# A modulation matrix loaded 32 rows at a time into four partition blocks, and summed in 12 products instead of 48

## The reference, cut to what matters

```python
ada = (jax.nn.silu(c) @ ada_w[l] + ada_b[l])[:, None, :]      # c: (1, 1024), ada_w: (1024, 6144)
sh1, sc1, g1, sh2, sc2, g2 = jnp.split(ada, 6, axis=-1)
u = rms_norm_2(h, norm1_g[l]) * (1 + sc1) + sh1
...
h = h + g1 * (merged @ w_out[l])
u2 = rms_norm_2(h, norm2_g[l]) * (1 + sc2) + sh2
h = h + g2 * peer_layer(u2, ...)
```

## Time and profile before

| | us |
|---|---|
| median of 3 runs | 1569.6 (1567.91 to 1569.87) |
| the profiled execution, its own time | 1573.47 |
| the span of its trace | 1571.5 |
| TensorE busy in the span | 1459.9 (93%) |
| the 32 modulation adds on DVE | 67.6 busy, 26.5 idle before them |
| the 32 modulation loads, issue to landing (median) | 6.4 |

### The profile page before, as it was taken

The page is one execution under the profiler, slowest core; times in us unless marked ns, Lnnn a source line. Parts: engine busy times, 40 slices in busy tenths (PEclk is TensorE's granted clock), DMA queues, the critical chain, the costliest instruction groups (busy, mean ns, idle before and its releaser), DMA issues.

```text
span 1571.5 us, 22748 instructions
## 1 busy us (share of the span) xinstructions
PE 1459.9 (93%) x8272; PEld 1120.8 (71%) x8272; DVE 1049.8 (67%) x2170; ACT 546.4 (35%) x1128; POOL 563.6 (36%) x382
## 2 busy tenths in 40 slices
PE   8999999999999999999999999998988988888777
PEld 7999998767999999998989985444444443333333
DVE  6655376875734328998976468785858585858556
ACT  5444353363544436443134242221212121212114
POOL 2455428220344441001002234554545444444451
PEclk9999999999999999999999999999999998999999
DMA  9888958996999997999976969999999999999996
GB/s 365 312 329 317 348 217 338 315 326 241 407 372 371 376 376 294 374 398 342 362 281 226 401 244 403 404 427 427 427 427 426 427 427 427 427 427 427 426 428 267
DMA packets 99814, 571.91 MB, mean 364 GB/s; under 512 B 11536, under 2 KB 11664, under 8 KB 50448
## 3 DMA queue, kind: packets, MB, share of 16 engines
q1 hardware_dynamic: 61056, 298.15, 51.3%
q0 software_dynamic: 37520, 268.47, 40.7%
q10 hardware_dynamic: 1152, 4.16, 0.7%
HBM read 569.67 MB, written 135.27 MB: 449 GB/s over the span
## 4 chain that ended last, share of the span: by engine, by line
PE 57%; DMA 26%; DVE 6%; SPq 5%; POOL 3%; issue 2%; ACT 1%; ACTq 0%; POOLq 0%; DVEq 0%
DMA arena<-pairs,eidx 15%; PE ps L2727 10%; PE ps L2113 8%; PE ps L2112 8%; PE ps L2111 8%; DMA ring<-pairs,eidx 6%; PE ps L2504 5%; SPq L664 3%; PE ps L2200 2%; PE ps L2198 2%; PE ps L2199 2%; DMA arena<-in_ada 2%; POOL w_lo L754 2%; SPq L663 2%; PE ps L2619 2%
## 5 line engine op out<-in xcount | busy, mean ns | idle before, releaser
L2727 PE MATMUL ps<-arena 128*128 128x512 f32 x844 | 402.6, 626 | 69.1 <-ACT arena L1252 69.1
L2727 PEld LDWEIGHTS ps<-arena 128*128 128x128 f32 x844 | 165.8, 201 | 289.0 <-issue 192.8
L1965 DVE CUSTOM_DVE_ANT_0 arena<-arena 128x1024 f32<-128x1024 f32 x211 | 255.2, 1225 | 145.3 <-DMA arena<-pairs,eidx 144.1
L822 POOL DMA_INDIRECT arena<-pairs,eidx x210 | 244.3, 1163 | 257.1 <-PE ps L2727 208.4
L754 POOL TENSOR_TENSOR w_lo<-ring,w_hi 128x1024 fp32r<-128x1024 f32 x76 | 207.9, 2738 | 257.7 <-DVE w_lo L1305 171.3
L2111 PE MATMUL ps<-u_hi,w_hi 128*128 128x256 f32 (+1 forms) x912 | 259.4, 284 | 1.8 <-POOL w_lo L754 1.5
L2113 PE MATMUL ps<-u_hi,w_lo 128*128 128x256 f32 (+1 forms) x912 | 259.6, 285 | 0.0
L2112 PE MATMUL ps<-u_lo,w_hi 128*128 128x256 f32 (+1 forms) x912 | 259.2, 284 | 0.0
L842 ACT ACTIVATE w_hi<-ring 128x1024 fp32r<-128x1024 f32 x188 | 197.8, 1056 | 149.7 <-PE ps L2200 71.2
L2111 PEld LDWEIGHTS ps<-u_hi,w_hi 128*128 128x128 f32 x912 | 172.1, 189 | 3.2 <-issue 2.3
L2113 PEld LDWEIGHTS ps<-u_hi,w_lo 128*128 128x128 f32 x912 | 172.3, 189 | 0.0
(11 more groups left out here) (394 smaller groups left out, 2505.3 us busy)
## 6 DMA issues: line engine op xcount, KB each, us to landing
ring<-in_stream SPq DMA_DIRECT2D x121, 1024.0 KB, 7.0
pairs<-in_peer_u SPq DMA_DIRECT2D x128, 512.0 KB, 7.5
pairs<-in_peer_v SPq DMA_DIRECT2D x128, 512.0 KB, 8.6
arena<-in_ada SPq DMA_DIRECT2D x32, 768.0 KB, 6.4
arena<-in_stream SPq DMA_DIRECT2D x8, 1024.0 KB, 9.9
arena<-pairs,eidx POOLq DMA_INDIRECT x210, 19.7
h<-in_x_t SPq DMA_DIRECT2D x2, 544.0 KB, 4.7
ring<-in_stream SPq DMA_DIRECT2D x2, 512.0 KB, 7.1
```

Of the source, the lines that this page charges most:

```text
L822: pool.indirect_dma_start(slot_of(n), None, pairs, own).then_inc(landing(n)[0], 16)
L1965: dve.tensor_tensor_reduce(row, row, hf[:, n % HEAD_ROWS // TOPK, :], 1.0, 0.0, ALU.mult, ALU.add, dots[:, n % HEAD_ROWS:n % HEAD_ROWS + 1 ...
L2727: mm = pe.matmul(ps[:, Y_BANKS[j // TOPK] + half, :], diag[:, n % DIAGS, :], slot_of(n)[:, D + half * 512:D + half * 512 + 512], start=(hd ...
```

## The change

Each load now brings 32 rows with all their 6144 columns. It reads the same four arrays of one `kt`, but 32 rows of each, and puts the four quarters of the columns below each other: partition `32 j + r` gets quarter `j` of row `r`. So every partition holds 1536 columns of a row, as before, and the DVE instruction has the same size, 128 x 1536. All 32 adds go into one accumulator of 1536 columns, and each waits for the one before it. `silu_c` has 32 columns, since the scalar of a partition now depends on which 32 rows are loaded. Four small loads on SP's queue put `c` into that form. After the last add each column block of 128 holds, in four groups of 32 partitions, partial sums of four different results; TensorE takes them apart with 12 products by `quarter`, a matrix with a one where row // 32 equals the column. DVE adds the bias to all 48 columns at one place.

The diff, with the functions that it touches:

```diff
+ADA_ROWS = P // ADA_Q
 CONSTS = [("ident", P), ...,
-          ("ones", P), ("rot", P), ("cos", T), ("sin", T), ("neg_mask", P)]
+          ("ones", P), ("rot", P), ("cos", T), ("sin", T), ("neg_mask", P), ("quarter", WIDE)]
+    quarter = np.zeros((P, ADA_Q), np.float32)
+    quarter[np.arange(P), np.arange(P) // ADA_ROWS] = 1.0
+    put("quarter", quarter)
-        silu_c = sb("silu_c", [P, KT])
+        silu_c = sb("silu_c", [P, KT * ADA_Q])
-        ada_acc = view(ADA_Q, ADA_W)
+        ada_acc = view(ADA_Q, ADA_W // ADA_Q)
+        ada_flat = ada_acc.rearrange("p q w -> p (q w)")
+        place(ADA_Q * ADA_W)
             def load_ada(kt, q):
                 sp.wait_ge(ada_step, kt * ADA_Q + (q + 3))
-                n = kt * ADA_Q + q
-                src = a["ada"][n] if isinstance(n, int) else a["ada"][bass.ds(n, 1)].rearrange("o p w -> p (o w)")
+                quarters = slice(kt * ADA_Q, kt * ADA_Q + ADA_Q) if isinstance(kt, int) else bass.ds(kt * ADA_Q, ADA_Q)
+                src = a["ada"][quarters, q * ADA_ROWS:(q + 1) * ADA_ROWS, :]
                 sp.dma_start(ada_ring[:, q % 2, :], src).then_inc(ada_in[q % 2], 16)
+            c_rows = a["cols"][:, COL["c"]:COL["c"] + KT].rearrange("(q r) k -> r q k", q=ADA_Q)
+            for g in range(ADA_Q):
+                own = silu_c[g * ADA_ROWS:(g + 1) * ADA_ROWS, :].rearrange("r (q k) -> r q k", q=ADA_Q)
+                sp.dma_start(own, c_rows).then_inc(c_in, 16)
-            act.activation(silu_c[:, :], V("c", 0, KT), ACT.Silu).then_inc(silu_c_done, 1)
+            act.wait_ge(c_in, 16 * ADA_Q)
+            act.activation(silu_c[:, :], silu_c[:, :], ACT.Silu).then_inc(silu_c_done, 1)
-            act.wait_ge(ada_done, 4)
+            act.wait_ge(ada_done, 3)
             def ada_add(kt, q):
                 dve.wait_ge(ada_in[q % 2], kt * 32 + (q // 2 * 16 + 16))
-                dve.wait_ge(ada_step, kt * ADA_Q + (q + 1))
-                dve.scalar_tensor_tensor(ada_acc[:, q, :], ada_ring[:, q % 2, :], silu_c[:, bass.ds(kt, 1)],
-                                         ada_acc[:, q, :], ALU.mult, ALU.add).then_inc(ada_step, 1)
+                dve.wait_ge(ada_step, kt * ADA_Q + (q + ADA_Q))
+                dve.scalar_tensor_tensor(ada_flat, ada_ring[:, q % 2, :], silu_c[:, bass.ds(q * KT + kt, 1)],
+                                         ada_flat, ALU.mult, ALU.add).then_inc(ada_step, 1)
             dve.wait_ge(ada_mm, 1)
-            then(dve.tensor_tensor(ada[:, 0:24], ps[:, 1, 0:24], V("ada_b", 0, 24), ALU.add), ada_done)
+            by_quarter = "p (q j) -> p q j"
+            sums = ps[:, 1, 0:48].rearrange("p (j q) -> p q j", q=ADA_Q)
+            then(dve.tensor_tensor(ada[:, :].rearrange(by_quarter, q=ADA_Q), sums, V("ada_b", 0, 48).rearrange(by_quarter, q=ADA_Q), ALU.add),
+                 ada_done)
             then(dve.scalar_tensor_tensor(gain1[:, :], ada[:, 8:16], 1.0, V("norm1", 0, KT), ALU.add, ALU.mult), ada_done)
+            then(dve.scalar_tensor_tensor(gain2[:, :], ada[:, 32:40], 1.0, V("norm2", 0, KT), ALU.add, ALU.mult), ada_done)
-            dve.wait_ge(ada_mm, 2)
-            then(dve.tensor_tensor(ada[:, 24:48], ps[:, 1, 24:48], V("ada_b", 24, 24), ALU.add), ada_done)
-            then(dve.scalar_tensor_tensor(gain2[:, :], ada[:, 32:40], 1.0, V("norm2", 0, KT), ALU.add, ALU.mult), ada_done)
-            def ada_sums(first, end):
+            def ada_sums():
                 pe.wait_ge(ada_step, KT * ADA_Q + ADA_Q)
-                flat = ada_acc.rearrange("p q w -> p (q w)")
-                for m in range(first, end):
-                    mm = pe.matmul(ps[:, 1, m:m + WIDE], flat[:, m * P:(m + 1) * P], C("ones")[:, 0:WIDE], start=True, stop=True)
+                for j in range(ADA_W // P):
+                    mm = pe.matmul(ps[:, 1, ADA_Q * j:ADA_Q * j + WIDE], ada_flat[:, j * P:(j + 1) * P], C("quarter"), start=True, stop=True)
                 mm.then_inc(ada_mm, 1)
-                                ada_sums(0, 24)
+                                ada_sums()
-                        if m + e == 1:
-                            ada_sums(24, 48)
-            pe.wait_ge(ada_done, 4)
```

More of the change, by code:

```diff
@@ L431, in program @@
         silu_c_done = sem("silu_c_done")
+        c_in = sem("c_in")
         sq_done = sem("sq_done")
```

## The result

The changed kernel takes 1732.5 us (median of 4 runs, 1723.4 to 1745.4), the kernel before 1569.6 us: the ratio is 1.104, 95% interval 1.099 to 1.108. It is slower by some 163 us, where the prediction said 100 us and a range up to 1715. Three executions in the chip's slower state are left out of all times and ratios here: one of the kernel before (2858 us), one of experiment 1's (1797 us) and one of experiment 2's (1754 us). The profiled execution is the shortest of the four, 1723.4 us, so the traces are compared at +150 us.

The account below looks back on a forecast made before the run. The prediction took TensorE (busy 93%) and the DMA engines as both near their limits, the later one varying by stage. 50 + 26 + 32 - 8 = +100 us gave 1670 us against the median; range 1620 to 1715 us.

Parts of the forecast that it names:

- The main mechanism: Modulation loads: a source with 4 outermost runs on four DMA engines, 7.37 us per load for 1.84; chance 0.72.
- The rival of sixteen or eight engines: Modulation loads spread wider, so faster: 1562 us with sixteen engines, about -4 us with eight; chance 0.14 together.
- Feed-forward 1: 20 to 206 us: four engines overloaded by 4.3 us a turn, 67 us less slack; +50 us, from +25 to +67.
- which leaves some 17 us to eat up: Feed-forward 1: ring loads issued four pieces of 6.0 us ahead, landing within 7 us, hide some 17 us.
- Projection: Input projection: six loads in turn with ring loads need 59 us for 33; +26 us, between +15 and +35.
- (2.45 + 7.37) x 6: Input projection: each of six turns takes a ring load's 2.45 us plus a modulation load's 7.37; 59 us.
- Last eight: Last eight modulation loads: 7.37 us each, last add at 427.4 us against 395.35; +32 us, between +28 and +36.
- Come no later: Feed-forward 2's first weights, queued behind the last eight loads on SP, land while the last is added.
- Sums: Two places of the sums on TensorE: twelve products for 48 take 2.65 us for 10.6; -8 us.
- both places lie on the chain with TensorE busy around them: Places of the sums: being on the chain of waits, their saved time is won in full, 8.0 us.
- The choked rival: SP stands at issues while four engines run dry, each load paying about 2.6 us; 1710 to 1755 us, chance 0.08.
- mostly hidden: Four engines, but feed-forward 1 costs nothing and the projection +10; +30 us, 1600 us, chance 0.06.

Follow-up runs that it names:

- experiment 1: The changed kernel with the input array reordered so that a load's source has 128 rows outermost; ratio to the kernel before 1.000.
- experiment 2: The kernel before with a spare row stored behind every 32, so each modulation load's source has 4 outermost; 1740.5 us, ratio 1.105.
- this stretch alone: The kernel before with 4 outermost only in the 8 modulation loads of the input projection; 1613.0 us, ratio 1.025.
- +36 alone: The kernel before with 4 outermost only in the last 8 modulation loads; 1608.0 us, ratio 1.023.

## Why the prediction was wrong, point by point

**The main mechanism held.** The load of 4 outermost runs on four engines: DMA share 0.25, adds 7.37 us apart, the whole loss gone with 128 outermost. The rule of the Trainium skill (DMA: Bandwidth & Descriptors, section Why a DMA increments its semaphore by 16 and not by 1) agrees with these rows on the number of engines; which four they are no row here shows. The rival of sixteen or eight engines fell for the kernel as changed.

**What failed is the size of three terms, and with the first two the range.**

*Feed-forward 1, +50 predicted, +80.5 measured.* The excess in each turn was right: the adds come 16.45 us apart on average (43.5 to 290.2 in 15 steps), for the 16.3 of the working. The step that failed is "which leaves some 17 us to eat up". First, the allowance was smaller: a ring load is not issued four pieces of 6.0 us ahead of its use. In the trace of before, the one issued at 37.65 us lands 7.1 us later and is split from 55.31 on, so it is 10.6 us early; later ones, such as the load issued at 82.86, are 10 us early. Second, it did not last some four turns but one and a half. Here is that piece's split, before and in the changed kernel, whose SP issued its load at 37.8 us:

```profile
55.31 1.05 ACT L842 ACTIVATE w_hi<-ring 128x1024 fp32r<-128x1024 f32 x1
```
```profile
60.38 1.06 ACT L853 ACTIVATE w_hi<-ring 128x1024 fp32r<-128x1024 f32 x1 [4.85 <-DMA ring<-in_stream]
```

It landed at 60.3 us, 15.6 later than before, behind only two modulation loads, for which the working had 2 x 5.5 = 11 us. From there on nothing is left to hide an excess: the adds slip by some 4 us a turn from the second on (58.1 us for 54.4, 74.9 for 66.5). Also, the kernel before did not need 12 us for each add: its last two stood together, at 208.1 and 209.8 us, and 15 steps took 166 us, not 180. With 16.45 us for each that is 247: +80. The upper end, 67, has no allowance in it, but took the same 12.0 and missed it too.

*Projection, +26 predicted, +47 measured (+41 with this stretch alone).* The step that failed is "(2.45 + 7.37) x 6": a turn took 12.2 us, not 9.8. It rests on engines that keep 26.7 GB/s whatever they write beside each other, and the four kept 21.5. Why they slow down stays open. Besides, the first of these loads was added 17.9 us after its issue (237.0 to 254.9 us with this stretch alone), for which the six turns left no room. The upper end of +35 was made of a smaller slowing.

*Last eight, +32 predicted, +25 in the changed kernel and +36 alone (+31 by the ends of the adds).* The 7.37 us are right. The start was earlier than thought in the changed kernel: 43 of the 86 table copies ahead of these loads are issued by the end of the 24th add, for 34 before, and the first of the eight is issued 66 us after that end, for 79. "Come no later" was wrong for the loads of feed-forward 2's weights: they hold up the last two modulation loads by 2 to 3 us each.

*Sums, -8 predicted, about nothing measured.* The step that failed is "both places lie on the chain with TensorE busy around them": that is no proof that a whole place's time is won. At the second place a DVE split stood right behind, covered by the sums themselves, and took 2.55 of the 5.3 us; the rest went to the 3.0 us by which the last add came later and to the clock, as far as one trace can tell. In the changed kernel the stages behind the last add are 2.8 us shorter.

*The rival "with eight engines"* would have been wrong by far if it had come: 8 outermost cost 78 us in the kernel before, where "about -4" with 8 us from the sums means +4. And "sixteen engines" would not have been free with 16 outermost.

*The choked rival* named the right size (1710 to 1755) by luck. A fixed part paid by every load is not seen: alone the loads follow each other at 7.37 us. The extra came from a slower turn where both kinds of load overlap, and from an allowance that was smaller and gone sooner.

*The rival "mostly hidden"* fell: feed-forward 1 hid nothing of its excess beyond the first two loads.

## What to carry to other kernels

Look at the outermost dimension of both sides of a load, as the built program has it: it decides how many engines carry it, and here also how well they do; 128 and 32 were at full speed, 16 and 8 were not. If the rows of a tile come from a few arrays, lay the array out in the order of the load rather than stepping through it. When a few engines are the bottleneck, work out each stretch as a rate from first to last transfer, and read the slack off the trace as the time from a landing to its use; and a gain of TensorE time counts only as far as what stands right behind it is ready.

## What the runs showed of the hardware

What a busy engine moves in the last eight loads, by the rate over 16 times the share:

| outermost of the source | share | GB/s | GB/s of a busy engine |
|---|---|---|---|
| 4 (changed kernel) | 0.25 | 103 | 26 |
| 8 | 0.49 | 144 | 18.4 |
| 16 | 0.78 | 171 | 13.7 |
| 32 (380 to 390 us) | 0.67 | 222 | 20.7 |
| 128 | 0.66 | 222 | 21.0 |

With 8 and 16 outermost the engines are slower than in the kernel before, with 32 they are not. If an engine gets a run of neighbouring groups, its rows are 32, 16 and 8 neighbours with 4, 8 and 16 outermost; how 32 and 128 are dealt out no run shows. Neighbours in one engine's share cannot be the whole cause, since with 4 outermost they are the most and a busy engine is at its fastest: how many engines work at once seems to count too. Nor do the runs say which side it is, because the rows that an engine reads in memory change together with the partitions that it writes.

The Trainium skill (SBUF — State Buffer, section Door 1: The DMA port swizzle) has partitions 0 to 3 and 32 to 35 on one port and 4 to 7, with 36 to 39, on another. By it eight neighbours lie on two ports, and engines that go through such groups side by side meet on the same port. That fits the kernels with 8 and 16 outermost, but with 4 outermost two engines with 32 rows each (0 to 31 and 32 to 63) would by it share all their ports, and there no engine is slowed (26 GB/s). No run here shows a port, so this is an explanation that fits in part and not one that was shown. The same may be why ring loads and modulation loads over four engines slow each other down (21.5 GB/s for 26.7); that was not tried by itself and stays open.

The traces also show DVE and POOL in each other's way: of a modulation add and a POOL split that overlap, the one that starts later took longer (add 4.00 us for 1.81, split 3.91 for 2.41), and a shift of 0.2 us changed which one it was.
